# Emitting the gate chains of the HGRN2 heads in pairs instead of one head at a time

## The reference

```
fq   = silu(hq)
f    = lb + (1.0 - lb) * sigmoid(hf)
logf = log(f);  kin = 1.0 - f
# per chunk of 64 tokens (8 for the sample group):
b = cumsum(logf)
o = (fq*exp(b)) @ S  +  causal[(fq*exp(b)) @ (kin*exp(-b)).T] @ v
S = exp(b_last) * S + (kin*exp(b_last - b)).T @ v
```

## Time and profile before

| | |
|---|---|
| median of the runs shown | 4162.87 us (2 runs: 3978.47 and 4347.26) |
| the profiled execution | 3975.19 us |
| its span on the slowest core | 3973.7 us (the eight cores: 3939.7 to 3973.7) |
| granted TensorE clock, mean | 0.838 of full speed |
| TensorE matmul busy | 2926.2 us (74%) |
| VectorE busy | 1568.5 us (39%) |
| ScalarE busy | 1040.7 us (26%) |
| DMA | 519.77 MB, 131 GB/s in the mean |

### The profile page before, as it was taken

How to read it: one execution, slowest core, us unless ns; L and a number is a source line. 1 busy time by engine, 2 the same in 40 slices (tenths; PEclk the granted TensorE clock), 3 DMA queues, 4 the chain that set the end, 5 groups by cost and what they waited for, 6 DMA issues and landing times.

```text
span 3973.7 us, 48452 instructions; the slowest of 8 cores (3939.7 to 3973.7 us)
## 1 busy us (share of the span) xinstructions
PE 2926.2 (74%) x14699; PEld 1403.0 (35%) x14699; DVE 1568.5 (39%) x3350; ACT 1040.7 (26%) x2205; POOL 218.7 (6%) x417
## 2 busy tenths in 40 slices
PE   5765987659785799659985798659965898568434
PEld 2322433224332344224432344224432443234323
DVE  0246233453136432462345333553256233543143
ACT  1052111521124211521133211521152113421221
POOL 0000000000000000000000000000000000000000
PEclk9886998769986799869996899769986999679757
DMA  9961786707854266505530253304530353125724
GB/s 185 160 126 44 140 196 140 158 22 161 201 140 100 70 169 226 158 5 159 208 151 23 85 179 134 122 31 139 218 122 11 122 213 124 64 70 166 273 74 145
DMA packets 99421, 519.77 MB, mean 131 GB/s; under 512 B 11456, under 2 KB 29632, under 8 KB 50368
## 3 DMA queue, kind: packets, MB, share of 16 engines
q0 software_dynamic: 59472, 438.59, 40.1%
q1 hardware_dynamic: 39696, 78.09, 6.0%
HBM read 564.22 MB, written 67.37 MB: 159 GB/s over the span
## 4 chain that ended last, share of the span: by engine, by line
PE 58%; DVE 16%; DMA 10%; issue 7%; ACT 7%; DVEq 1%; SPq 1%; ACTq 0%; POOL 0%; POOLq 0%
PE ps L553 16%; PE ps L534 14%; PE ps L539 13%; PE ps L671 7%; DMA wst<-w13a 4%; DMA wst<-scr_w13a 2%; DVE Sf L1017 2%; PE ps L723 2%; DVE Sb L1014 2%; PE ps L1030 1%; DVE xres L474 1%; DVE xres L485 1%; PE ps L459 1%; DMA wst<-w13b 1%; PE ps L1002 1%
## 5 line engine op out<-in xcount | busy, mean ns | idle before, releaser
L534 PE MATMUL ps<-xT,wst 128*128 128x512 bf16 (+1 forms) x3168 | 732.6, 377 | 165.3 <-DMA wst<-w13a 63.8
L546 DVE TENSOR_TENSOR hT<-sil,ps 128x512 bf16<-128x512 f32 (+1 forms) x396 | 254.7, 643 | 1229.5 <-PE ps L539 1175.2
L539 PE MATMUL ps<-xT,wst 128*128 128x512 bf16 (+1 forms) x3168 | 707.2, 368 | 1.6 <-DVE hT L546 1.6
L553 PE MATMUL ps<-Wbig,hT 128*128 128x512 bf16 x2904 | 635.9, 380 | 0.0
L544 ACT ACTIVATE sil<-ps 128x512 f32<-128x512 f32 (+1 forms) x396 | 222.3, 562 | 1151.9 <-PE ps L534 1127.3
L534 PEld LDWEIGHTS ps<-xT,wst 128*128 128x128 bf16 x3168 | 306.2, 102 | 525.3 <-issue 217.5
L539 PEld LDWEIGHTS ps<-xT,wst 128*128 128x128 bf16 x3168 | 306.0, 101 | 346.5 <-issue 24.0
L553 PEld LDWEIGHTS ps<-Wbig,hT 128*128 128x128 bf16 x2904 | 283.2, 98 | 336.0 <-issue 1.6
L671 PE MATMUL ps<-xT,wst 128*128 128x512 bf16 (+1 forms) x1584 | 373.1, 398 | 22.9 <-ACT xT L461 11.2
L671 PEld LDWEIGHTS ps<-xT,wst 128*128 128x128 bf16 x1584 | 155.7, 107 | 234.7 <-issue 110.2
L474 DVE SCALAR_TENSOR_TENSOR xres<-ps,xres 128x512 f32<-128x512 f32 x198 | 136.3, 688 | 245.6 <-PE ps L553 204.9
(11 more groups left out here) (185 smaller groups left out, 2475.0 us busy)
## 6 DMA issues: line engine op xcount, KB each, us to landing
wst<-scr_w13a POOLq DMA_DIRECT2D x73, 1024.0 KB, 7.6
wst<-scr_w13b POOLq DMA_DIRECT2D x73, 1024.0 KB, 5.3
wst<-scr_win POOLq DMA_DIRECT2D x41, 1024.0 KB, 6.7
Wbig<-scr_w2a POOLq DMA_DIRECT2D x26, 1408.0 KB, 10.4
Wbig<-scr_w2b POOLq DMA_DIRECT2D x26, 1408.0 KB, 14.9
lnbuf<-lnp SPq DMA_DIRECT2D x54, 512.0 KB, 4.4
wst<-w13a POOLq DMA_DIRECT2D x26, 1024.0 KB, 17.8
wst<-w13b POOLq DMA_DIRECT2D x26, 1024.0 KB, 10.4
```

The lines of the kernel that those rows point to most:

```text
L534: S.op("pe", lambda e, kc=kc, c=c, slot=slot, bg=bg: e.matmul(ps[bg][:, 0:N], lhsT=wst[slot][:, kc * 512 + c * 128:kc * 512 + (c + 1) * 12 ...
L539: S.op("pe", lambda e, kc=kc, c=c, slot=slot, bu=bu: e.matmul(ps[bu][:, 0:N], lhsT=wst[slot][:, kc * 512 + 256 + c * 128:kc * 512 + 256 + ...
L546: S.op("dve", lambda e, si=si, bu=bu, j=j: e.tensor_tensor(out=hT[:, j, 0:N], in0=sil[si][:, 0:N], in1=ps[bu][:, 0:N], op=ALU.mult), reads ...
L553: S.op("pe", lambda e, j=j, h=h, m=m, pr=pr: e.matmul(ps[pr[h]][:], lhsT=hT[:, j, m * 128:(m + 1) * 128], rhs=Wbig[:, j * 1024 + h * 512:j ...
```

## The change

The function b2_chain(h), called behind every cast of piece 4, becomes b2_pair(h0), called behind the casts of c = 1 and c = 3 for heads (0, 1) and (2, 3). The same operations on the same tiles are emitted in another order: both Ln; then tensor_scalar and scan of the first head and of the second; then the two exponentials and the EBL copy of the first head and of the second; then the two products of the first head and of the second. Nothing is added or removed, and the buffers are the same.

```diff
--- before.py
+++ after.py
@@ -635,28 +635,41 @@
         mask = cst[:, C_SCAN + 128:C_SCAN + 256] if is_s else msk512[:, 0:N]
         mkeys = ["cst"] if is_s else [("msk512", r) for r in range(4)]
 
-        def b2_chain(h):
-            t1 = T1h[h]
-            if h % 2 == 0:
-                t2, t3, k2_, k3_ = rbuf[:, 0:N], rbuf[:, 512:512 + N], ("rbuf", 0), ("rbuf", 1)
-            else:
-                t2, t3, k2_, k3_ = sil[1][:, 0:N], xb.bitcast(F32)[:, 0:N], ("sil", 1), "xb"
-            S.op("act", lambda e: e.activation(out=t2, in_=t1[:, 0:N], func=AF.Ln, bias=lbv[:, h:h + 1], scale=lbv[:, 4 + h:5 + h]),
-                 reads=T1K[h] + ["lbv"], writes=[k2_])
-            S.op("dve", lambda e: e.tensor_scalar(out=t1[:, 0:N], in0=t1[:, 0:N], scalar1=lbv[:, 8 + h:9 + h], scalar2=lbv[:, 4 + h:5 + h],
-                                                  op0=ALU.mult, op1=ALU.add),
-                 reads=T1K[h] + ["lbv", k2_], writes=T1K[h])
-            S.op("dve", lambda e: e.tensor_tensor_scan(out=t3, data0=mask, data1=t2, initial=0.0, op0=ALU.mult, op1=ALU.add),
-                 reads=[k2_] + mkeys, writes=[k3_])
-            S.op("act", lambda e: e.activation(out=t2, in_=t3, func=AF.Exp), reads=[k3_], writes=[k2_])
-            S.op("act", lambda e: e.activation(out=t3, in_=t3, func=AF.Exp, scale=-1.0), reads=[k3_], writes=[k3_])
-            S.op("dve", lambda e: e.tensor_tensor(out=hT[:, 8 + h, 0:N], in0=hq_s[:, h, 0:N], in1=t2, op=ALU.mult),
-                 reads=[("hq_s", h), k2_], writes=[("hT", 8 + h)])
-            S.op("dve", lambda e: e.tensor_tensor(out=hT[:, 12 + h, 0:N], in0=t1[:, 0:N], in1=t3, op=ALU.mult),
-                 reads=T1K[h] + [k3_], writes=[("hT", 12 + h)])
+        def b2_pair(h0):
+            hs = (h0, h0 + 1)
+            bufs = {}
+            for h in hs:
+                if h % 2 == 0:
+                    bufs[h] = (rbuf[:, 0:N], rbuf[:, 512:512 + N], ("rbuf", 0), ("rbuf", 1))
+                else:
+                    bufs[h] = (sil[1][:, 0:N], xb.bitcast(F32)[:, 0:N], ("sil", 1), "xb")
+            for h in hs:
+                t1 = T1h[h]
+                t2, t3, k2_, k3_ = bufs[h]
+                S.op("act", lambda e, h=h, t1=t1, t2=t2: e.activation(out=t2, in_=t1[:, 0:N], func=AF.Ln, bias=lbv[:, h:h + 1], scale=lbv[:, 4 + h:5 + h]),
+                     reads=T1K[h] + ["lbv"], writes=[k2_])
+            for h in hs:
+                t1 = T1h[h]
+                t2, t3, k2_, k3_ = bufs[h]
+                S.op("dve", lambda e, h=h, t1=t1: e.tensor_scalar(out=t1[:, 0:N], in0=t1[:, 0:N], scalar1=lbv[:, 8 + h:9 + h], scalar2=lbv[:, 4 + h:5 + h],
+                                                             op0=ALU.mult, op1=ALU.add),
+                     reads=T1K[h] + ["lbv", k2_], writes=T1K[h])
+                S.op("dve", lambda e, t2=t2, t3=t3: e.tensor_tensor_scan(out=t3, data0=mask, data1=t2, initial=0.0, op0=ALU.mult, op1=ALU.add),
+                     reads=[k2_] + mkeys, writes=[k3_])
             nl = N // per
-            S.op("act", lambda e: e.copy(out=EBL[:, h, 0:nl], in_=t2.rearrange("p (c s) -> p c s", s=per)[:, :, per - 1]),
-                 reads=[k2_], writes=[("EBL", h)])
+            for h in hs:
+                t2, t3, k2_, k3_ = bufs[h]
+                S.op("act", lambda e, t2=t2, t3=t3: e.activation(out=t2, in_=t3, func=AF.Exp), reads=[k3_], writes=[k2_])
+                S.op("act", lambda e, t3=t3: e.activation(out=t3, in_=t3, func=AF.Exp, scale=-1.0), reads=[k3_], writes=[k3_])
+                S.op("act", lambda e, h=h, t2=t2: e.copy(out=EBL[:, h, 0:nl], in_=t2.rearrange("p (c s) -> p c s", s=per)[:, :, per - 1]),
+                     reads=[k2_], writes=[("EBL", h)])
+            for h in hs:
+                t1 = T1h[h]
+                t2, t3, k2_, k3_ = bufs[h]
+                S.op("dve", lambda e, h=h, t2=t2: e.tensor_tensor(out=hT[:, 8 + h, 0:N], in0=hq_s[:, h, 0:N], in1=t2, op=ALU.mult),
+                     reads=[("hq_s", h), k2_], writes=[("hT", 8 + h)])
+                S.op("dve", lambda e, h=h, t1=t1, t3=t3: e.tensor_tensor(out=hT[:, 12 + h, 0:N], in0=t1[:, 0:N], in1=t3, op=ALU.mult),
+                     reads=T1K[h] + [k3_], writes=[("hT", 12 + h)])
 
         pbanks = (0, 1, 7)
         nchunk = 0
@@ -692,7 +705,8 @@
                     S.op("act", lambda e, c=c, b=b: e.activation(out=T1h[c][:, 0:N], in_=ps[b][:, 0:N], func=AF.Sigmoid), reads=pk, writes=T1K[c])
                 elif p == 4:
                     S.op("dve", lambda e, c=c, b=b: e.tensor_copy(out=hT[:, 4 + c, 0:N], in_=ps[b][:, 0:N]), reads=pk, writes=[("hT", 4 + c)])
-                    b2_chain(c)
+                    if c % 2 == 1:
+                        b2_pair(c - 1)
                 else:
                     S.op("act", lambda e, c=c, b=b: e.activation(out=G[:, c, 0:N], in_=ps[b][:, 0:N], func=AF.Silu), reads=pk, writes=[("G", c)])
             if not is_s:
```

## The result

The changed kernel is 0.88% faster: against the kernel before the ratio is 0.9912, with a 95% interval of 0.9898 to 0.9927, which is 29 to 41 us. The profiled execution took 3939.96 us, where that of before took 3975.19 and the forecast was 3940. The medians over all executions are 3948.04 us (13 runs) and 4027.39 us (10 runs before, where two were shown ahead). They lie apart from the profiled times because some executions of either kernel had the four cores of a die at a lower clock, and the ratio leaves these out.

The account below looks back on a forecast made before the run. TensorE's matmul queue was taken to bound the kernel, standing idle in piece 4 behind gate chains on VectorE and ScalarE. Eight tiles at 4.2 us (33.6) plus 2.6 took 36 us off 3975.2, giving 3940, range 3920 to 3978.

Parts of the forecast that it names:

- the sum: Whole kernel: 33.6 us from eight prompt tiles plus 2.6 from the sample tile, 36 us off the profiled 3975.2, giving 3940.
- The start of the first pair: Piece 4, heads 0 and 1: first scan at about 2518.5, 1.9 us later than now, as the price of the pair.
- The clock behind the gap: Sixteen matmuls behind TensorE's gap: still slowed, 5.3 to 5.8 us, so no term was put for them.
- The second pair: Piece 4, heads 2 and 3: both Ln hidden with 0.5 us or more to spare, L605 4.3 us earlier.
- The sample tile: Its gate chains, 128 columns wide, end about 2.6 us earlier, and the load L767 moves with them.
- The wait for L605: TensorE's transpose L880 waiting for the copy L605: falls from 119.3 to about 84 us, longest from 13.1 to about 10.
- (a): Stage A, first four tiles: the DMA queue sets the time, 4 x 4.2 us return as weight waits, 3956 us; chance 0.12.
- (b): Behind the gap: TensorE stays at 2.4 GHz, sixteen matmuls take 3.63 us, 16 us more gained, 3923 us; chance 0.05.
- (c): Gate chains: pairs don't overlap as written, each keeps a hole, 15 to 20 us are won, 3957 us; chance 0.07.
- (e): Gate chains: order changes nothing, since something else ahead of L605 sets the gap, 3975 us; chance 0.03.
- (d): Gate chains: scans beside exponentials slow each other; at 35% longer operations each tile loses 1.4 us, 3986 us; chance 0.03.
- the choice against the rule: VectorE in piece 4: operations overlap by the trace's spacings; full lengths would cost 1.9 us a tile, about 3954 us.

Follow-up runs that it names:

- e1: Kernel before, its serial chains called two at a time behind the casts of c = 1 and c = 3, without overlap: ratio 1.0022, profiled 3985.77 us.
- g3: Changed kernel with only heads 2 and 3 as a pair, heads 0 and 1 in their own chains: ratio 0.9939 to the kernel before, profiled 3953.47 us.
- e2: Changed kernel with every scan issued twice, same input and output tile: no ratio, profiled 3986.41 us.
- e9: Changed kernel with prompt_attn_c(1) ahead of pair (2, 3) and the products of heads 2 and 3 behind prompt_attn_b(2): ratio 0.9872 to the kernel before, profiled 3925.36 us.
- g1: Changed kernel with 36 useless matmuls put into TensorE's gap in each prompt tile: ratio 0.9903 to the kernel before, profiled 3932.69 us.
- e3: Changed kernel with the Ln of each odd head issued twice: ratio 0.9934 to the kernel before, profiled 3948.39 us.

## Why the prediction was right, and where not

**The step that failed.** It is in the sum: the forecast is "made against the profiled execution", with the words "I forecast a run like the profiled one", while the median shown for the kernel before was 4162.87 us. 3940 lies 222.9 us, or 5.4%, under that median. The working of the change has 36 us. The other 187 us are the choice of the run, and no term of the sum stands for them. The runs show that the change has no part in them: over more executions the medians are 4027.39 before and 3948.04 after, and the ratio of like runs is 0.9912, a change of 0.88% or 35 us. Read against the median that stood there, the forecast change is six times what the change does.

**The mechanism was right.** 36 us were forecast off 3975.2, and 35 came. That the holes between scan and product are what the pairs take out is shown by e1 (overlap away, gain away) and g3 (half of the pairs, half of the holes); that VectorE's work then sets the length of the stretch is shown by e2. That the total agrees within 1 us is in part luck. Three terms of the sum were off, and the execution profiled after reached its first projection 4.3 us later than the one before (221.46 and 217.19 us), ahead of anything that the change touches. From the first projection of the first tile to that of the sample tile it gained 38.6 us where 33.6 were forecast, and behind that only 0.9 where 2.6 were.

**The start of the first pair.** The forecast has the first scan 4.2 us behind the g = 0 products (2518.5 against 2514.35). It stands there (4.1 to 4.2 us) in three tiles, and at 5.9 us in the five others. The term left out is TensorE's clock in piece 4: the two L936 stand behind sixteen matmuls, and these took 5.31 us in those five tiles, but in only one tile before. Those tiles gained 2.6 to 2.9 us in the stretch and the three others 4.3 to 4.5, where 4.3 were forecast for each. The change doesn't decide this by itself: e9, whose program is the same up to the first pair, has the late scan in one tile of eight.

**The clock behind the gap.** The forecast put no term for it, expecting 5.3 to 5.8 us for the sixteen matmuls there. They took 4.90 to 5.16 us in six tiles and 6.09 and 6.19 in the others, 5.3 in the mean after 5.5 before: outside the range on both sides, and worth 2.0 us in all. Slow groups (4.9 to 5.3 us instead of 3.63) stand ahead of the gap too: before in piece 3 of four tiles and in piece 4 of one, after in piece 3 of two tiles and in piece 4 of five. The two fewer in piece 3 gave back 3.4 us. So the 38.6 us of the tiles are 27.3 of the stretch, 3.4 and 2.0 of these groups, and 5.9 from places that no run here singles out. g1 shows that work in the gap doesn't remove the slow matmuls; what sets which sixteen are slow stays open.

**The second pair.** From the first scan to L605 the forecast had 11.2 us and the trace has 10.99. The cover of the two Ln was right in size (0.5 us). But the forecast names no reason why the Ln of head 3 should matter to the tensor_scalar of head 2, and there is one, the shared name that e3 shows.

**The sample tile** gave 2.4 of the 2.6 us forecast in its stretch, but to the end of the program only 0.9 were left (246.6 to 245.7 us from its first projection). The forecast put nothing for a DMA that takes it back, and looked only at the weights. The load L767 did start 2.6 us sooner, counted from the tile's first projection, but the load of ck_in, issued before it, stayed where it was, and TensorE's wait for it grew by 2.1 us.

**The wait for L605** was forecast to fall to about 84 us, and it fell to 100.5. The forecast took the 35 us off this wait, though its own working has the gap at 10.4 us. The eight gaps went from 103.7 to 83.6 us in the sum, 20 us less and not 35; the rest of the gain is that the gap also begins earlier. The sum didn't use this number. Nor is this wait the largest of TensorE's list: before, L459 waits 169.3 us for xb and L1030 140.6 us for osq.

**The rivals.** (a) The gain hidden by weights: no, the waits of stage A stayed, and tiles 2 to 4 gained as much as the later ones. (b) A clock that stays up behind the gap: not seen (4.9 to 6.2 us, not 3.63). (c) and (e): the timeline rules both out. (d) VectorE and ScalarE slowing each other: a scan is 1.22 us beside an exponential as it is alone. The spacings (product to product 0.58 to 0.61 us at lengths of 0.67 to 0.69) also bear out the choice against the rule that one operation waits until the pipe is flushed.

## What to carry to other kernels

Where an engine stands idle for short waits on another inside a chain of small operations, and a second chain with its own buffers is at hand, put the two side by side and count the work of the busier engine: the stretch can't become shorter than that sum, and here it came down to it (16.1 us) in three tiles and within 1.7 us of it in the others. A long wait in a list is worth its length only if no second string is as late; try one edit on each string and both together before dropping either. Ahead of moving an eviction, look up which later matmuls need its bank. And state a forecast against the same time of before that it will be read against: where that time is a median of few and far apart executions, forecast the ratio.

## What the runs showed of the hardware that was not expected

TensorE's clock dropped behind waits as short as 2.3 us, and not each time. In the changed kernel the granted clock was 1.00 (2.4 GHz) during the wait of 2.28 us that ends at 2489.24, and 0.68 in the mean over the sixteen matmuls from 2489.92 on, which ran in 5.31 us instead of 3.63. In the sixth tile of the kernel before, the same wait of 2.28 us was followed by sixteen matmuls at the full clock. In g1 it was 1.00 over 7.7 us of matmuls and over the wait of 2.62 us behind them, and then 0.69 over the fifteen that took 5.21 us. The mean granted clock moved by 0.002 between the two kernels (0.838 and 0.840), so it doesn't show where the slow ones stand. The Trainium skill (TensorE: Matmul & The Clock Gate, The HAM clock gate) says that activity releases the clock. The trace of g1 has 7.7 us of matmuls ahead of a short wait, and the clock fell behind it all the same.
